# A fifth buffer for the experts' down weights, one buffer for gathered rows and one for output rows

## What is computed

```python
def hier_moe(h, ...):            # 4 groups of 8 experts, hidden width 256
    gtop, gsel = lax.top_k(glog, 1)            # the best group of a token
    etop, esel = lax.top_k(elog_g, TOP_K)      # its best two experts
    ew = jax.nn.softmax(etop, axis=-1) * gp
    ...
    for gi in range(N_GROUPS):
        a = jnp.einsum('btd,edf->btef', h, w_e_gate[gi])
        u = jnp.einsum('btd,edf->btef', h, w_e_up[gi])
        act = jax.nn.silu(a) * u * combine[..., gi, :, None]
        out = out + jnp.einsum('btef,efd->btd', act, w_e_down[gi])
```

## Time and profile before

| | us |
|---|---|
| runs | 1253.7, 1254.6, 1257.23 |
| median | 1254.6 |
| profiled execution, its own time | 1250.49 |
| its span, first to last instruction | 1248.8 |
| mean granted clock of TensorE | 0.939 of full |

### The profile page before, as it was taken

How to read it: one execution, slowest core, us unless ns; L and a number is a source line. 1 busy time by engine, 2 the same in 40 slices (tenths; PEclk the granted TensorE clock), 3 DMA queues, 4 the chain that set the end, 5 groups by cost and what they waited for, 6 DMA issues and landing times.

```text
span 1248.8 us, 14760 instructions
## 1 busy us (share of the span) xinstructions
PE 1107.5 (89%) x5886; PEld 728.9 (58%) x5886; DVE 510.4 (41%) x1099; ACT 214.3 (17%) x505; POOL 142.2 (11%) x298
## 2 busy tenths in 40 slices
PE   4899998999999998899699999999964998978756
PEld 2344777777788876788277777774431333332212
DVE  3102504356775485474824455543345111110015
ACT  2100000442421122365110100000110110100001
POOL 3000400000303000013200000000011111111001
PEclk9899999999999999799599999999985999998887
DMA  9977542242323333221653322149546999999954
GB/s 358 284 220 197 174 73 70 35 117 57 68 68 68 85 69 79 49 68 53 193 171 116 58 78 68 68 144 246 222 180 246 384 420 416 418 419 419 415 198 178
DMA packets 93086, 226.30 MB, mean 181 GB/s; under 512 B 21278, under 2 KB 39951, under 8 KB 78782
## 3 DMA queue, kind: packets, MB, share of 16 engines
q1 hardware_dynamic: 83270, 202.70, 49.8%
q10 hardware_dynamic: 4624, 12.75, 2.9%
q0 software_dynamic: 5120, 9.88, 2.2%
HBM read 210.60 MB, written 23.08 MB: 187 GB/s over the span
## 4 chain that ended last, share of the span: by engine, by line
PE 32%; SPq 6%; DMA 6%; DVE 3%; issue 2%; ACT 1%; POOL 0%; POOLq 0%; ACTq 0%; DVEq 0%
PE ps L1730 15%; PE ps L2115 5%; DMA w_gate_up<-w_e_up 5%; PE ps L1772 5%; SPq L2281 4%; PE ps L555 3%; PE ps L2133 2%; SPq L2290 2%; PE ps L2358 1%; PE ps L2105 1%; PE ps L1792 1%; PE ps L1763 1%; DVE y_pairs L2374 0%; DMA y_pairs<-pair_scratch 0%; DMA x_gathered<-h_scratch,toks 0%
## 5 line engine op out<-in xcount | busy, mean ns | idle before, releaser
L555 PE MATMUL ps<-hT,w_ring 128*128 128x288 f32 x1408 | 352.0, 410 | 11.9 <-PEq L106 10.0
L555 PEld LDWEIGHTS ps<-hT,w_ring 128*128 128x128 f32 x1408 | 267.2, 192 | 85.1 <-issue 13.5
L2115 PE MATMUL ps<-w_gate_up,xT 128*64 128x512 f32 x528 | 132.5, 642 | 23.0 <-DMA w_gate_up<-w_e_up 21.6
L2115 PEld LDWEIGHTS ps<-w_gate_up,xT 128*64 128x64 f32 x528 | 41.5, 147 | 111.7 <-issue 82.2
L2261 DVE TENSOR_TENSOR act<-silu_gate,ps 128x256 f32<-128x256 f32 x17 | 7.2, 422 | 201.3 <-ACT silu_gate L2076 201.3
L2133 PE MATMUL ps<-w_down,actT 128*64 128x512 f32 x264 | 62.1, 598 | 8.8 <-DVE actT L2265 8.8
L405 PE MATMUL ps<-w_ring,hT 128*128 128x512 f32 x128 | 58.3, 615 | 3.0 <-DMA w_ring<-w_in 3.0
L1299 DVE SCALAR_TENSOR_TENSOR conv_y<-z_staged,convT,conv_y 128x512 f32<-128x512 f32 x72 | 54.1, 752 | 2.6
L1295 DVE TENSOR_SCALAR conv_y<-z_staged,convT 128x512 f32<-128x512 f32 x24 | 11.8, 493 | 90.7 <-ACT z_staged L843 85.8
L405 PEld LDWEIGHTS ps<-w_ring,hT 128*128 128x128 f32 x128 | 24.9, 197 | 33.8 <-issue 30.0
L2133 PEld LDWEIGHTS ps<-w_down,actT 128*64 128x64 f32 x264 | 18.0, 136 | 41.2 <-issue 29.1
(11 more groups left out here) (455 smaller groups left out, 1558.6 us busy)
## 6 DMA issues: line engine op xcount, KB each, us to landing
w_ring<-w_in SPq DMA_DIRECT2D x16, 2048.0 KB, 14.1
w_gate_up<-w_e_gate SPq DMA_DIRECT2D x32, 1024.0 KB
w_gate_up<-w_e_up SPq DMA_DIRECT2D x32, 1024.0 KB
w_down<-w_e_down SPq DMA_DIRECT2D x32, 1024.0 KB, 25.6
w_ada_slots<-w_ada SPq DMA_DIRECT2D x10, 2048.0 KB, 9.1
w_ring<-w_ada SPq DMA_DIRECT2D x2, 2048.0 KB, 12.3
w_ring<-w_pa SPq DMA_DIRECT2D x2, 2048.0 KB, 13.6
w_ring<-w_pb SPq DMA_DIRECT2D x2, 2048.0 KB, 8.0
```

Source lines behind the costliest of these rows:

```text
L555: last = nc.tensor.matmul(psum[:, bank + hf, 0:HALF], w[:, c, 128 * q:128 * q + 128], x[:, c, HALF * hf:HALF * hf + HALF], start=c == 0, s ...
L2115: last = te.matmul(psum[side(u), s % 2, :], xT[:, s % 2, c, side(u)], gu[s % GU_BUFS][:, u, :, c, :], start=c == 0, stop=c == KC - 1)
```

## The change

WD_BUFS goes from 4 to 5: a fifth buffer w_down4 lies at base + 69632. For this the two halves of xg become one, and so do those of yo, which moves to a place that h2T had in the merge stage; fin_ss moves behind the new buffer, and the routing tables move down by 4 KB a partition. The new buffer still overlaps routing tables, so SP waits for a new semaphore, wdone, which DVE's last routing instruction raises, and then loads step 4's down weights. In the loop SP now loads the down weights of step s+5 once down(s) is done.

With one xg, gather(s) waits until x_transposes(s-1) are done, and POOL's order becomes gather(0) and then for each s gather(s+1), scatter(s). With one yo, ACT's copy of step s waits for scatter(s-1). Each of the two pairs of semaphores becomes one.

```diff
--- before.py
+++ after.py
@@ -1510,7 +1510,7 @@
 LONE_AT = 8
 FIXED = NE // 2 + 1
 STEPS = (NE + OVER_BLOCKS) // 2
-GU_BUFS, WD_BUFS = 3, 4
+GU_BUFS, WD_BUFS = 3, 5
 BIG = 1e30
 ROUTE_CONST = 64
 ROUND = 12582912.0
@@ -1550,7 +1550,7 @@
     base = m.merge_base = ring + 88704
     m.gu = [weights("w_gate_up0", ring + 51200), weights("w_gate_up1", ring + 16384),
             weights("w_gate_up2", base)]
-    m.wd = [rows("w_down0", base + 32768), rows("w_down1", ring), rows("w_down2", base + 103616), rows("w_down3", base + 87232)]
+    m.wd = [rows("w_down0", base + 32768), rows("w_down1", ring), rows("w_down2", base + 103616), rows("w_down3", base + 87232), rows("w_down4", base + 69632)]
     m.kept_rows = base
     m.y_base = ring
     tail = Region(nc, base + 96448)
@@ -1955,10 +1955,11 @@
     sb = Region(nc, m.merge_base + 49152)
     ac = sb("act", [128, 2, DE])
     sb = Region(nc, m.merge_base + 51200)
-    xg = sb("x_gathered", [128, 2, D])
+    xg = sb("x_gathered", [128, D])
     xT, aT = sb("xT", [128, 2, KC, 128]), sb("actT", [128, 2, 2, 128])
     routing = Region(nc, sb.offset)
-    yo = sb("y_block", [128, 2, D])
+    sb("routing_tables", [128, 2 * D])
+    yo = Region(nc, m.spare[1])("y_block", [128, D])
     sg = Region(nc, m.spare[0])("silu_gate", [128, 2, DE])
     em = routing("em", [128, NT, NE])
     one = routing("one", [128, 2, NT, NE])
@@ -1982,12 +1983,14 @@
     m.all_scattered = sem("all_scattered")
     h2d, h2tr, h2st, ld = (m.merged[n] for n in ("h2d", "h2tr", "h2st", "ld"))
     bothd, hotd, tabd, overd = sem("both_done"), sem("onehot_done"), sem("table_done"), sem("over_done")
+    wdone = sem("pair_weights_done")
     desc, onesr = m.rc[:, 0:32], m.rc[:, 32:64]
     strict, onesb = m.rcb[:, 0:128], m.rcb[:, 128:256]
     low, high = m.rcb[:, 256:266], m.rcb[:, 266:276]
     gu, wd = m.gu, m.wd
-    m.fin_ss = sb("fin_ss", [128, NT])
-    gth, sct = ([sem(f"{n}{i}") for i in range(2)] for n in ("gathered", "scattered"))
+    m.fin_ss = Region(nc, m.merge_base + 86016)("fin_ss", [128, NT])
+    assert sb.offset <= m.merge_base + 87232
+    gth, sct = sem("gathered"), sem("scattered")
     xtr, xev, gmm, sgd, acd, atr, aev, dmm, yev = (sem(n) for n in (
         "moe_xtr", "moe_xev", "moe_gu", "moe_silu", "moe_act", "moe_atr", "moe_aev", "moe_down", "moe_yev"))
     side = lambda u: slice(CAP * u, CAP * u + CAP)
@@ -2005,6 +2008,8 @@
     def sync(sp):
         sp.wait_ge(overd, 1)
         load_down(sp, m, ins, 3, (6, 7))
+        sp.wait_ge(wdone, 1)
+        load_down(sp, m, ins, 4, (8, 9))
 
         def experts(s):
             pair = block_pair(s)
@@ -2032,33 +2037,31 @@
         pool.wait_ge(h2tr, NT)
         pool.wait_ge(h2st[0], 48)
         pool.wait_ge(h2st[1], 32)
-        p.memset(xg[:, :, :], 0.0).then_inc(ps, 1)
+        p.memset(xg[:, :], 0.0).then_inc(ps, 1)
         pool.wait_ge(ps, 1)
         last_tok, last_pair = p.to_reg(TOK - 1), p.to_reg(2 * TOK - 1)
 
         def gather(s):
-            if s >= 2:
-                pool.wait_ge(xtr, s - 1)
-            p.indirect_dma_start(out=xg[:, s % 2, :], out_offset=None, in_=m.h2_dram[:, :],
+            if s >= 1:
+                pool.wait_ge(xtr, s)
+            p.indirect_dma_start(out=xg[:, :], out_offset=None, in_=m.h2_dram[:, :],
                                  in_offset=bass.IndirectOffsetOnAxis(ap=m.toks[:, block_pair(s):block_pair(s) + 1], axis=0),
-                                 bounds_check=last_tok, oob_is_err=False).then_inc(gth[s % 2], 16)
+                                 bounds_check=last_tok, oob_is_err=False).then_inc(gth, 16)
 
         def scatter(s):
             pool.wait_ge(yev, s + 1)
             p.indirect_dma_start(out=m.y_dram[:, :], out_offset=bass.IndirectOffsetOnAxis(ap=m.pairs[:, block_pair(s):block_pair(s) + 1], axis=0),
-                                 in_=yo[:, s % 2, :], in_offset=None,
-                                 bounds_check=last_pair, oob_is_err=False).then_inc(sct[s % 2], 16)
+                                 in_=yo[:, :], in_offset=None,
+                                 bounds_check=last_pair, oob_is_err=False).then_inc(sct, 16)
 
         def run(lo, hi):
             pool.wait_ge(tabd, 4)
             gather(lo)
-            gather(lo + 1)
             for s in range(lo, hi):
-                if s + 2 < hi:
-                    gather(s + 2)
+                if s + 1 < hi:
+                    gather(s + 1)
                 scatter(s)
-            for i in range(2):
-                pool.wait_ge(sct[i], 16 * ((hi + 1 - i) // 2))
+            pool.wait_ge(sct, 16 * hi)
         all_steps(pool, run)
         p.memset(m.fin_ss[:, :], 1.0).then_inc(m.all_scattered, 1)
 
@@ -2075,9 +2078,9 @@
                     act.wait_ge(acd, s - 1)
                 a.activation(sg[:, s % 2, :], psum[:, s % 2, 0:DE], ACT.Silu).then_inc(sgd, 1)
                 act.wait_ge(dmm, s + 1)
-                if s >= 2:
-                    act.wait_ge(sct[s % 2], 16 * (s // 2))
-                a.copy(yo[:, s % 2, :].rearrange("p (a d) -> p a d", a=2), psum[:, 4:6, :]).then_inc(yev, 1)
+                if s:
+                    act.wait_ge(sct, 16 * s)
+                a.copy(yo[:, :].rearrange("p (a d) -> p a d", a=2), psum[:, 4:6, :]).then_inc(yev, 1)
         all_steps(act, run)
 
     def tensor(pe):
@@ -2098,11 +2101,11 @@
         last.then_inc(pt, 1)
 
         def x_transposes(s):
-            pe.wait_ge(gth[s % 2], 16 * (s // 2 + 1))
+            pe.wait_ge(gth, 16 * (s + 1))
             if s >= 1:
                 pe.wait_ge(xev, s)
             for c in range(KC):
-                last = te.transpose(psum[:, 2 + c // 4, 128 * (c % 4):128 * (c % 4) + 128], xg[:, s % 2, c::KC], m.ident[:, :])
+                last = te.transpose(psum[:, 2 + c // 4, 128 * (c % 4):128 * (c % 4) + 128], xg[:, c::KC], m.ident[:, :])
             last.then_inc(xtr, 1)
 
         def gate_up(s):
@@ -2244,7 +2247,7 @@
         step(v.tensor_scalar(mx[:, :], m.w[:, :, 1], 1.0, None, ALU.add))
         tt(mx[:, :], mx[:, :], gsum[:, :], ALU.mult)
         step(v.reciprocal(m.w[:, :, 0], mx[:, :]))
-        tt(m.w[:, :, 1], m.w[:, :, 1], m.w[:, :, 0], ALU.mult)
+        v.tensor_tensor(m.w[:, :, 1], m.w[:, :, 1], m.w[:, :, 0], ALU.mult).then_inc(wdone, 1)
 
         def x_evacuate(s):
             dve.wait_ge(xtr, s + 1)
```

## The result

The changed kernel takes 1299.65 us in the median of four runs (1295.66 to 1302.37), against 1254.3 before. The ratio is 1.0354 with a 95% interval of 1.0322 to 1.0386: slower by 3.5%. I had said 1309, range 1264 to 1342. The profiled run took 1302.37 us, 51.9 more than the one of before.

What follows compares the result with a forecast made beforehand. Before, DMA bound later steps (16.9 us each); afterwards the gather chain: twelve periods of 19.55, three of 14, last step 12.7, plus 56.9 us in all. This gives 1307.4 from the profiled run, 1311.5 from the median; said 1309, range 1264 to 1342.

Steps and rivals of the forecast that it cites:

- D(1): End of the down product of step 1 in the expert stage; near 993.6 us was a sign of being right.
- Periods: Expert-stage time per step, end of one down product to the next: 8.35 + 9.5 + 1.7 = 19.55 us, twelve times.
- The landing G: Time of a gather from issue to landing, on the path of each step: taken as 9.5 us, range 8.0 to 11.1.
- The clock term: Extra time per step because PE's clock drops in its wait for the gather: 1.7 us, bounds 0 and 4.9.
- a sign of being wrong: Gathers landing in 8 us or less, x transposes on time, or output copies waiting for the scatter.
- The last three gathers: Gathers 14 to 16 meet little traffic, landing in 4.8 to 6.7 us: periods of 14 us, three of them 42.
- D(16) - D(0): From the end of step 0's down product to step 16's; the latter forecast at 1263.5 us, against 1206.6.
- Rival C: Waits keep PE's clock at 1.2 GHz in the whole step: period about 22.3 us, time about 1345; chance 13%.
- Rival B: DMA and gather chain meet, landing about 8 us, clock holds: period 16.6, about 1271 us, edge 1264; chance 16%.
- Rival D: Step 4's down load behind the pair weights comes too late for the DMA hole; no share of its own.
- One output buffer: Next output copy waits for the scatter, done by 10.6 us after the down product, wanted at 12.5: cost nothing.
- the stage would end 5.0 us sooner: Fifth down buffer's 2 MB load fits the 6.8 us DMA hole; gain 5.0 us if DMA still bound, not subtracted.

Runs made afterwards that it cites:

- The order experiment: Changed kernel with its single gather buffer, but POOL issues the gather of step s+2 ahead of scatter s: 1249.42 us, ratio to the kernel before 0.9971.

## Why the prediction was right

*The mechanism.* Each link stood in the profile after as written: gather behind scatter in POOL's order, 2.64 us from the start of the copy to its issue (2.69 said, from the product's end 0.05 us earlier), x transposes released by the gather, D(1) at 996.9 (993.6 said). PE's waits at the x transposes in the first twelve of these steps sum to 52.3 us, where I had said some 60, of 4 to 6 us each; they run from 2.7 to 7.1. (The 59.9 us above hold the last three as well, so their nearness to 60 is chance.) The order experiment shows the mechanism to be the cause.

*Periods.* Said 19.55 us for the first twelve, found 18.7. The landing G of gathers 2 to 13 is 8.5 us in the mean (6.9 to 11.2); I said 9.5. I had put it between 4.8 and 10.2 by DMA's share of 0.87. The share was 0.92, and that way would have given 9.8: what counts is the load that runs beside the gather, as the kernels with cut loads show, not the mean share. The clock term was 1.9 us in the mean (transposes to D: 6.93 to 8.50 instead of 5.62), said 1.7. So the landing is the mis-sized term: 12 x 1.0 = 12 us too much, of which the clock takes 2 back. And 18.7 us is a mean of two kinds: seven of the twelve steps last 16.7 to 17.5 us, five last 19.7 to 22.3. Seven of these gathers land in 7.9 us or less, and landings of 8 us or less I had named as a sign of being wrong. The mean stays in the forecast's range through the five long steps; I had not foreseen two kinds, so that it fits is in part luck.

*The last three gathers.* Said 14 us each, found 12.9, 14.7 and 20.0. The first met an almost idle DMA (landing 4.6), the second the end of the last gate-and-up load (6.4; DMA share 0.98 in its first 2.7 us). The third met the loads of the end stage, which SP issues from 1221.79 to 1227.94, and landed in 9.1. I had counted this gather among those that meet little traffic. The three together are 47.5 us, not 42. That this 5.5 us too little stands against 10.4 too much in the twelve periods is luck.

*Sum.* 12.5 for the last step, 12.7 said. D(16) - D(0): said 289.3, found 284.2. From the profiled run of before this gives 1250.5 + 51.8 = 1302.3, which is what the profiled run of after took. The median is 2.7 lower. My 1309 lay between this way of adding and the one from the median of before, which gave 1311.5. Rival C (the clock low for the whole step) fell: it came back in each step. Rival B (periods of 16.6) was too quick by 2 us a step in the mean, though the seven short steps are nearly its own. Rival D: the load did go into the hole.

*One output buffer, fifth buffer.* The first cost nothing, as said. For the second I wrote that the stage would end 5.0 us sooner were DMA still the bound. That step was wrong, though it did not enter the sum: before the change PE waits for gate-and-up loads, and these did not move. With the gather out of the way 3.4 to 3.6 us came, of which the steps show 1.3 to 1.4 and the time behind D(16) about 1. The profiled runs as a whole do not show the gain (spans of 1249.0 and 1250.3 us, before 1248.8), as their D(0) lies 2.5 and 3.8 us later. It rests on the medians, and where its rest comes from stays open.

*The page on the gather's time.* The fit of the Trainium skill, DMA: Bandwidth & Descriptors, "Anatomy of one DMA — SWDGE (gpsimd) path", gave an estimate of 3.2 us for a gather of 128 rows. The trace comes near it only where no large load runs beside the gather: 3.3 to 4.7 us there, 1.02 of it POOL's own instruction, for 40 to 106 rows. Beside the weights it disagrees: a median of 7.9 in the changed kernel and 10.2 before, and 7.9 and 9.8 for the single row of step 8. With 3.2 in my sum the change would have been free.

## What to carry to other kernels

Before a double buffer becomes a single one, write down the order of the queue that refills it: what counts is not when the buffer comes free, but which waiting instruction stands ahead of the refill on its engine. Here a transfer for the next step stood behind one that waits for the end of this step, and so closed a loop through four engines and a DMA; issued ahead of it, the same single buffer costs nothing. And before a buffer is added, ask which of several streams the waiting engine waits for; here a lead in one did not help the other until the order of loads handed it on.

## What I had not expected of the hardware

A gather took 3.3 to 4.7 us with no large load beside it, 6 to 7.5 with part of one, 9 to 11 with weights all along its way; how many rows it fetches hardly shows beside that (9.8 us for one row of 4 KB, 10.2 in the median). And a shorter step did not simply give a shorter sum: whether loads were cut or the clock was kept up, steps began to alternate between short and long (12.5 and 16 to 18 us with light down loads), with light down loads because a quick step brings the big load closer to the next gather (with the clock kept up, that reason was not tested). A term that is taken out of such a loop comes back in part in another.
